# Layer norm of a fused two-layer backbone step: sums by token tile in column groups, root and reciprocal on 96x128, result spread by one-row products

## The chip, the cores and the metric

The kernel runs on one core of a Trainium2 chip. Its engines are TensorE (PE in the profile; PEld is its loading of weights), VectorE (DVE), ScalarE (ACT), GpSimd (POOL) and SyncE (SP); each runs its own list of instructions in order and they meet by semaphores. The metric is the device time of one execution in microseconds (us), and the median of several runs is compared.

## What is computed

A step of a diffusion backbone with two layers for 384 tokens (128 of a prompt, 256 of a latent) of width 1024, all in float32. The layer, cut to what matters:

```python
def layer_norm(x, g, b):
    mu = jnp.mean(x32, axis=-1, keepdims=True)
    var = jnp.mean(jnp.square(x32 - mu), axis=-1, keepdims=True)
    return (x32 - mu) * lax.rsqrt(var + LN_EPS) * g + b

def trunk_layer(x, mod, p, ...):
    shift1, scale1, gate1, shift2, scale2, gate2 = split(mod, 6)
    y, k, v = token_mixer(x * (1 + scale1) + shift1, p, ...)   # projection, attention, pooling, convolution
    x = layer_norm(ALPHA * x + gate1 * y, p['ln1_g'], p['ln1_b'])
    u = x * (1 + scale2) + shift2
    return layer_norm(ALPHA * x + gate2 * hier_moe(u, p), p['ln2_g'], p['ln2_b'])
```

`hier_moe` sends each token to two of 32 gated experts, whose weights are read from memory in each layer. `mod` is a row of SiLU(cond) times `w_mod`, 6144 wide.

## The kernel before

**Layout.** Activations lie turned: `xT` and `uT` hold eight tiles (m = 0 to 7) of 128 channels (partitions) by T = 384 tokens (columns). So a sum over channels is a sum over partitions and over eight tiles, and TensorE makes it: a product with a 128x128 matrix of ones (`C["ones"]`) adds up the partitions and gives the same sum in every partition of a PSUM bank. `ln_t` is a scratch of ten 128x384 tiles. PSUM (`ps`) has eight banks of 512 columns. In the trace each float32 product is two matmul instructions, and a transpose is one.

**A normalisation.** There are two in each layer (`which` 0 and 1), four in all. VectorE (`residual_norm`, L1624) makes z = gate * y + scaled x in place in `uT`, tile after tile (L1640), and adds tiles 0 to 6 together (L1647). TensorE (`layer_norm`, L991) makes the mean from this sum (L994) and the last tile (L996). VectorE subtracts it from each tile, reading PSUM (L1655); ScalarE (`squares_root`) squares each tile (L1331); TensorE adds the squares, eight products of 384 columns (L1003); ScalarE takes the root on 128x384, for which it loads another function table (L1333); VectorE takes the reciprocal on 128x384 (L1662) and scales the eight tiles into `xT` (L1666).

**What follows it.** Next comes u = x * (1 + scale) + shift, even tiles on ScalarE (L1216), odd tiles on VectorE (L1453, `new_u`, after all eight scalings). The shift and scale come from the modulation product (`mod_product`, L796): for each k of eight, four products of 256 or 512 columns with 32-column weights that lie in four column groups of the array. ScalarE copies the result out (L1222), TensorE turns it (`mod_turn`, L808), VectorE adds the bias (L1441) and folds the norm's bias into the shift (L1618, L1621). In the first normalisation TensorE's order is: mean, steps k=0,1 of part 2, squares, steps 2 to 7 of part 2, half of part 3, the turn, the rest of part 3, and then the router product (L1028) on the new u. The first normalisation is followed by routing and the experts (chunks: L1074, L1066, L1081), the second, in layer 0, by the projection of layer 1 (L834), and in layer 1 by the output: ScalarE adds the bias (L1419), TensorE turns the tiles (L1193), both other engines copy them out (L1853, L1423), SyncE stores them. In the second normalisation of layer 0 the modulation product of the next layer (part 0) takes the place of part 2.

**Weights.** SyncE issues the loads into four slots of a ring and a fifth in the arena, each when its slot is free: the w_mod and w_in slots of the next layer behind the last experts (L521, L510), experts behind `gu_ready` and `down_done` of the chunk five before (L559, L561, L566).

## Time and profile before

| | us |
|---|---|
| three runs | 1105.05, 1108.22, 1108.25 |
| median | 1108.22 |
| span of the profiled execution, first to last instruction | 1105.3 |
| TensorE busy in it | 931.0 (84%) |
| VectorE, ScalarE, GpSimd busy | 384.5, 236.6, 178.5 |
| moved by DMA | 321.9 MB, mean 291 GB/s |

The profile is of one execution, and no time of that execution other than its span is given. All times of rows are counted from the span's start. A matmul's end is modelled, since matmuls are pipelined: two that follow each other overlap in their durations, so a group's length divided by its count is the better measure of their rate.

### The profile page before, as it was taken

To read this page: it belongs to the slowest core of one execution; us is meant where nothing else is said; L and a number is where in the kernel's file an instruction comes from. 1 tells how busy PE (TensorE), PEld (TensorE's weight loads), DVE (VectorE), ACT (ScalarE), POOL (GpSimd) and SP (SyncE) were. 2 spreads that over 40 slices of the span, in tenths; PEclk is the share of its full clock that TensorE was granted. 3 is DMA by queue.
4 is the path that set the end of the run, shared out by engine and by line. 5 is a ranking of instruction groups with operands and counts; after the bars stand their busy time and mean duration, and the time that the engine had idled before them with its cause. 6 is when DMAs were issued, how large, how long until landed. Compare 5 with 4: busy or idle time off the path is not lost.

```text
span 1105.3 us, 13927 instructions
## 1 busy us (share of the span) xinstructions
PE 931.0 (84%) x5252; PEld 549.7 (50%) x5252; DVE 384.5 (35%) x921; ACT 236.6 (21%) x565; POOL 178.5 (16%) x214
## 2 busy tenths in 40 slices
PE   4899988994899987798899998899489997779884
PEld 2356455543555543454445654554355554445453
DVE  0257554255211111111646846325611111111146
ACT  1200067032111110111230016703311111011104
POOL 5000000002322222222020000000322222222100
PEclk8899989996999998999999998999699999999998
DMA  9981154078799999997997215317789999999941
GB/s 358 378 308 36 81 193 207 4 293 345 299 412 414 414 413 412 411 386 312 380 336 286 84 41 231 160 41 300 294 339 412 415 414 412 348 415 410 414 182 58
DMA packets 73568, 321.88 MB, mean 291 GB/s; under 512 B 13198, under 2 KB 17638, under 8 KB 49184
## 3 DMA queue, kind: packets, MB, share of 16 engines
q1 hardware_dynamic: 58688, 295.72, 67.3%
q0 software_dynamic: 14816, 25.29, 6.3%
q8 instruction: 42, 0.69, 0.2%
q14 instruction: 22, 0.18, 0.0%
HBM read 321.46 MB, written 23.59 MB: 312 GB/s over the span
## 4 chain that ended last, share of the span: by engine, by line
PE 62%; DMA 16%; SPq 8%; DVE 8%; ACT 3%; issue 3%; POOLq 0%; ACTq 0%; DVEq 0%; POOL 0%
PE ps L834 13%; PE ps L1066 13%; DMA ring<-in_w_up 11%; PE ps L1016 7%; PE ps L1081 6%; PE ps L837 4%; SPq L559 3%; DMA ring<-in_w_mod 3%; SPq L561 2%; PE ps L796 2%; SPq L566 2%; PE ps L1003 2%; PE ps L1074 1%; DMA arena<-u_rows,row_idx 1%; PE ps L1090 1%
## 5 line engine op out<-in xcount | busy, mean ns | idle before, releaser
L1066 PE MATMUL ps<-ring,tail 128*64 128x256 f32 x1760 | 205.1, 384 | 10.4 <-DMA ring<-in_w_up 8.5
L1066 PEld LDWEIGHTS ps<-ring,tail 128*64 128x64 f32 x1760 | 144.0, 139 | 82.9 <-issue 24.5
L834 PE MATMUL ps<-uT,ring 128*128 128x384 f32 x448 | 149.7, 492 | 3.7 <-ACT uT L1216 3.7
L1795 DVE TENSOR_TENSOR arena<-arena,ps 128x128 f32<-128x128 f32 x68 | 19.6, 288 | 364.8 <-ACT arena L1366 364.8
L834 PEld LDWEIGHTS ps<-uT,ring 128*128 128x128 f32 x448 | 85.5, 192 | 60.3 <-issue 5.3
L1081 PE MATMUL ps<-ring,krow 128*64 128x512 f32 x408 | 103.6, 627 | 3.0 <-issue 2.2
L693 POOL DMA_INDIRECT y_pairs<-tail,row_idx x58 | 57.7, 995 | 289.6 <-ACT tail L1391 277.9
L1391 ACT ACTIVATE tail<-ps 128x512 f32<-128x512 f32 x58 | 34.6, 597 | 189.4 <-PE ps L1081 189.4
L688 POOL DMA_INDIRECT arena<-u_rows,row_idx x66 | 68.8, 1043 | 38.0 <-issue 20.1
L1513 DVE SCALAR_TENSOR_TENSOR arena<-arena,dw 128x414 f32<-128x414 f32 x118 | 67.7, 645 | 0.0
L1366 ACT ACTIVATE arena<-ps 128x128 f32<-128x128 f32 x68 | 18.8, 277 | 214.2 <-PE ps L1066 198.0
L1016 PE MATMUL ps<-arena,ring 128*128 128x384 f32 x192 | 62.2, 486 | 0.0
L1074 PE MATMUL ps<-cst,arena 128*128 128x128 f32 x272 | 42.3, 285 | 21.6 <-DMA arena<-u_rows,row_idx 17.8
L1790 DVE COPY tail<-ps 128x512 f32<-128x512 f32 x68 | 46.6, 691 | 37.5 <-PE ps L1074 30.0
L796 PE MATMUL ps<-ring,sT 128*32 128x512 f32 (+1 forms) x512 | 51.2, 540 | 8.5 <-DMA ring<-in_w_mod 8.5
L1128 PE MATMUL ps<-cst,arena 128*128 128x128 f32 x62 | 20.3, 328 | 42.9 <-DVE arena L1795 42.9
L1640 DVE SCALAR_TENSOR_TENSOR uT<-ps,modT,uT 128x128 f32<-128x128 f32 x64 | 23.5, 411 | 83.4 <-PE ps L1016 74.5
L1081 PEld LDWEIGHTS ps<-ring,krow 128*64 128x64 f32 x408 | 29.8, 140 | 41.3 <-issue 41.3
L1066 PE MATMUL ps<-arena,tail 128*64 128x256 f32 x416 | 49.2, 389 | 0.1
L1016 PEld LDWEIGHTS ps<-arena,ring 128*128 128x128 f32 x192 | 36.5, 190 | 25.4
L1074 PEld LDWEIGHTS ps<-cst,arena 128*128 128x128 f32 x272 | 32.1, 146 | 26.9 <-issue 20.9
L1066 PEld LDWEIGHTS ps<-arena,tail 128*64 128x64 f32 x416 | 36.4, 142 | 17.3 <-issue 7.5
(268 smaller groups left out, 979.6 us busy)
## 6 DMA issues: line engine op xcount, KB each, us to landing
ring<-in_w_gate SPq DMA_DIRECT2D x55, 1024.0 KB, 17.1
ring<-in_w_up SPq DMA_DIRECT2D x55, 1024.0 KB, 22.9
ring<-in_w_down SPq DMA_DIRECT2D x55, 1024.0 KB, 23.0
ring<-in_w_mod SPq DMA_DIRECT2D x12, 3072.0 KB, 11.2
arena<-in_w_gate SPq DMA_DIRECT2D x13, 1024.0 KB, 18.3
arena<-in_w_up SPq DMA_DIRECT2D x13, 1024.0 KB, 24.6
arena<-in_w_down SPq DMA_DIRECT2D x13, 1024.0 KB, 25.1
ring<-in_w_mod SPq DMA_DIRECT2D x6, 2048.0 KB, 15.9
```

Source lines behind the costliest of these rows:

```text
L688: pool.indirect_dma_start(xg[:, b, :], None, u_rows, bass.IndirectOffsetOnAxis(ap=idx, axis=0), bounds_check=2 * T - 1, oob_is_err=False). ...
L693: pool.indirect_dma_start(y_pairs, bass.IndirectOffsetOnAxis(ap=idx, axis=0), rows, None, bounds_check=4 * T - 1, oob_is_err=False).then_i ...
L796: last = mm(ps[32 * g_:32 * (g_ + 1), bank, 0:n], sT[:, 2 * k:2 * k + 32], mod_w[MOD_SLOTS[j][u]][:, row, off + g_ * n:off + (g_ + 1) * n] ...
L834: last = mm(ps[:, n % 4, 0:T], slot[s][:, k, c:c + P], uT[:, k, :], start=(k == 0), stop=(k == KD - 1))
L837: last = mm(ps[:, n % 4, 0:AW], uT[:, k, rows * P:(rows + 1) * P], slot[s][:, k, c:c + AW], start=(k == 0), stop=(k == KD - 1))
L1016: last = mm(ps[:, m % 4, 0:T], wt, mixT[:, k, :], start=(k == 0), stop=(k == KD - 1))
L1066: last = mm(ps[W * half:W * (half + 1), b, 0:2 * P].rearrange("p (j f) -> p j f", j=2), xc[:, b, k, :], gate_up_w[s][:, :, k, half * P:(ha ...
L1074: last = tr(ps[:, 5 + b, c * P:(c + 1) * P], xg[:, buf, c * P:(c + 1) * P], ident)
L1081: last = mm(ps[W * half:W * (half + 1), 3 + b, :], hT[:, b, f * W:(f + 1) * W], down_w[s][:, f, half * 512:(half + 1) * 512], start=(f == ...
L1391: fn(yrow[:, i % 2, :], ps[:, 3 + i % 2, :], ID).then_inc(y_rows.sem, 1)
L1513: conv_own.append(own.add(v.scalar_tensor_tensor(cacc[:, c, :], src, wt, cacc[:, c, :], ALU.mult, ALU.add)))
L1790: v.tensor_copy(xc[:, b].rearrange("p (h j) n -> p j h n", h=2), ps[:, 5 + b, :].rearrange("p (j h n) -> p j h n", j=4, h=2)).then_inc(sig ...
```

## The change

**First normalisation (which = 0).** The mean is made as before. The squares are added by `sum_by_tile`: for each m three products of 128 columns, one for each token tile, with 32 columns of ones as weights, in three column groups of the array; they write partitions 0 to 95 of one bank, 128 columns, so token tile g stands in the 32 partitions from 32g. Root and reciprocal work on 96x128. `spread` then multiplies one row of ones with one row of the result for each token tile and so fills banks 1 to 3, and VectorE scales from these three banks. Steps k = 2, 3, 4 of the modulation product are put between the squares' sums, k = 5, 6 behind them, and k = 7 and three steps of part 3 behind the spread. VectorE makes the odd tiles of u between the scalings.

**Second normalisation (which = 1).** The additions of L1647 go; the mean is summed by token tile too, straight from z, copied out by ScalarE with the factor -1/D, and spread to three banks; VectorE centres by an addition from there. The modulation's step 2 stands between the squares and steps 3 to 7 behind the spread. The modulation's bias is added after all eight scalings, not after the sixth. The output's turns use other banks.

The core of the diff:

```diff
+        stat = ln_t[0:32 * NT, 1, 0:2 * P].rearrange("p (b n) -> p b n", b=2)
...
+                def sum_by_tile(bank, x, m):
+                    for g_ in range(NT):
+                        last = mm(ps[32 * g_:32 * (g_ + 1), bank, 0:P], C["ones"][:, 0:32], x[:, g_ * P:(g_ + 1) * P],
+                                  start=(m == 0), stop=(m == KD - 1), tile_position=(0, 32 * g_))
+                    return last
+                def spread(rows):
+                    for g_ in range(NT):
+                        last = mm(ps[:, 1 + g_, 0:P], C["ones"][32 * g_:32 * g_ + 1, :], rows[32 * g_:32 * g_ + 1, :],
+                                  start=True, stop=True)
+                    last.then_inc(stat_spread.sem, 1)
...
                 def layer_norm(which):
-                    wait(z_summed, l, which + 1)
-                    mm(ps[:, 4 * (1 - which), 0:T], C["ones"], ln_t[:, 0, :], start=True, stop=False)
...
+                    if which:
+                        for m in range(KD):
+                            wait(z_ready, l, KD + m + 1)
+                            last = sum_by_tile(0, uT[:, m, :], m)
+                        last.then_inc(norm_sums.sem, 1)
+                        wait(stat_rows, l, 2)
+                        spread(stat[:, 0, :])
...
+                    if ahead < DEPTH:
+                        mod_product(ahead, part, 7, range(2))
                     for m in range(KD):
                         wait(squared, l, which * KD + m + 1)
-                        last = mm(ps[:, 5 - 4 * which, 0:T], C["ones"], ln_t[:, 2 + m, :], start=(m == 0), stop=(m == KD - 1))
-                    last.then_inc(norm_sums.sem, 1)
+                        last = sum_by_tile(5 - which, ln_t[:, 2 + m, :], m)
+                        if m == KD - 1:
+                            last.then_inc(norm_sums.sem, 1)
+                        if ahead < DEPTH and m in ((4,) if which else (2, 4, 6)):
+                            mod_product(ahead, part, 7, range(1 + m // 2, 2 + m // 2) if not which else range(2, 3))
+                    if not which:
+                        mod_product(ahead, part, 7, range(5, 7))
+                    wait(stat_rows, l, 2 * which + 1)
+                    spread(stat[:, 1, :])
...
-                mod_product(l, 2, 7, range(2, KD))
-                mod_product(l, 3, 4, range(KD // 2))
+                mod_product(l, 2, 7, range(KD - 1, KD))
+                mod_product(l, 3, 4, range(KD // 2 - 1))
                 mod_turn(l, 2, 7, D // 4)
-                mod_product(l, 3, 4, range(KD // 2, KD))
+                mod_product(l, 3, 4, range(KD // 2 - 1, KD))
...
                 def squares_root(which):
+                    if which:
+                        wait(norm_sums, l, 3)
+                        fn(stat[:, 0, :], ps[0:32 * NT, 0, 0:P], ID, scale=-1.0 / D).then_inc(stat_rows.sem, 1)
...
-                    fn(ln_t[:, 1, :], ps[:, 5 - 4 * which, 0:T], ACT.Sqrt, bias=epsc[:], scale=1.0 / D).then_inc(root_ready.sem, 1)
+                    fn(stat[:, 0, :], ps[0:32 * NT, 5 - which, 0:P], ACT.Sqrt, bias=epsc[0:32 * NT, :], scale=1.0 / D).then_inc(
+                        root_ready.sem, 1)
...
-                        if 1 <= m < KD - 1:
+                        if not which and 1 <= m < KD - 1:
...
+                        if which:
+                            v.tensor_tensor(by_tile(uT[:, m, :]), spread_rows, by_tile(uT[:, m, :]), ALU.add).then_inc(centred.sem, 1)
...
-                    own.add(v.reciprocal(ln_t[:, 0, :], ln_t[:, 1, :]))
-                    after(own.n)
+                    v.reciprocal(stat[:, 1, :], stat[:, 0, :]).then_inc(stat_rows.sem, 1)
+                    wait(stat_spread, l, 2 * which + 1)
...
+                    if which == 0:
+                        for m in range(4):
+                            scaled(m)
+                        mod_add(l, 2, 7, D // 4)
+                        own.add(mod_scale(l, 3, SC2))
+                        mod_fold("ln1_b", SH2, SC2)
+                        wait(mod_done, l, 2)
+                        next_u(1)
+                        scaled(4)
+                        scaled(5)
+                        next_u(3)
+                        scaled(6)
+                        scaled(7)
+                        next_u(5)
+                        next_u(7)
...
-                    last = tr(ps[:, 2 + n, m * P:(m + 1) * P], uT[:, 4 * h + m, t * P:(t + 1) * P], ident)
+                    last = tr(ps[:, (4 + n) % 8, m * P:(m + 1) * P], uT[:, 4 * h + m, t * P:(t + 1) * P], ident)
```

`DVE_STEPS`, the count of VectorE's own steps in a layer, goes from 209 to 202, and GpSimd's one-time signal for its zeroed block shares the semaphore of another zeroing.

## Rows read from the trace of the kernel before

**Rows 1.** The page, section 4: the chain that ended last, share of span by engine.
```profile
PE 62%; DMA 16%; SPq 8%; DVE 8%; ACT 3%; issue 3%; POOLq 0%; ACTq 0%; DVEq 0%; POOL 0%
```

**Rows 2.** Timeline, first normalisation of layer 0: start us, us, engine line operation, count [idle before].
```profile
232.49 3.77 ACT L1331 ACTIVATE arena<-uT 128x384 f32<-128x384 f32 x8 [39.90 <-DVE uT L1655]
233.07 5.43 PE L1003 MATMUL ps<-arena,cst 128*128 128x384 f32 x16 [0.20 <-ACT arena L1331]
...
236.28 1.28 ACT L1333 ACT_TABLE_LOAD   x1
238.43 4.04 PEld L796 LDWEIGHTS ps<-ring,sT 128*32 128x32 f32 x80 [0.55 <-issue]
238.43 4.52 PE L796 MATMUL ps<-ring,sT 128*32 128x256 f32 x80
238.53 0.58 ACT L1333 ACTIVATE arena<-ps,epsc 128x384 f32<-128x384 f32 x1 [0.97 <-PE ps L1003]
239.15 2.55 DVE L1662 RECIPROCAL arena<-arena 128x384 f32<-128x384 f32 x1 [3.28 <-ACT arena L1333]
...
241.73 1.68 DVE L1666 SCALAR_TENSOR_TENSOR xT<-uT,vec,arena 128x384 f32<-128x384 f32 x3
...
242.88 0.44 PE L808 MATMUL ps<-cst,pool_sums 128*128 128x128 f32 x2
...
243.25 1.93 PE L796 MATMUL ps<-ring,sT 128*32 128x256 f32 x32
...
244.19 3.62 ACT L1216 ACTIVATE uT<-xT,modT 128x128 f32<-128x128 f32 x8 [2.52 <-DVE modT L1621]
...
247.44 4.71 PE L1028 MATMUL ps<-uT,router_w 128*36 128x384 f32 x14 [1.31 <-DVE uT L1453]
```

**Rows 3.** Timeline, second normalisation of layer 0.
```profile
535.77 4.85 PE L1180 MATMUL ps<-cst,arena 128*128 128x128 f32 x42
...
536.06 1.39 DVE L1640 SCALAR_TENSOR_TENSOR uT<-ps,modT,uT 128x128 f32<-128x128 f32 x4 [4.86 <-PE ps L1180]
...
544.34 0.91 PE L994 MATMUL ps<-arena,cst 128*128 128x384 f32 x2 [3.72 <-DVE arena L1647]
...
546.48 3.81 DVE L1655 SCALAR_TENSOR_TENSOR uT<-ps,uT 128x384 f32<-128x384 f32 x8 [1.54 <-PE ps L996]
...
554.68 5.36 PE L796 MATMUL ps<-ring,sT 128*32 128x512 f32 x48
...
563.43 20.88 PE L834 MATMUL ps<-uT,ring 128*128 128x384 f32 x64 [2.02 <-ACT uT L1216]
```

**Rows 4.** Timeline, second normalisation of layer 1, the end of the program.
```profile
1071.94 5.52 PE L1180 MATMUL ps<-cst,arena 128*128 128x128 f32 x48
...
1084.15 3.81 DVE L1655 SCALAR_TENSOR_TENSOR uT<-ps,uT 128x384 f32<-128x384 f32 x8 [2.37 <-PE ps L996]
...
1093.98 4.32 DVE L1666 SCALAR_TENSOR_TENSOR xT<-uT,vec,arena 128x384 f32<-128x384 f32 x8
1094.63 4.32 ACT L1419 ACTIVATE uT<-xT,vec 128x384 f32<-128x384 f32 x8 [3.27 <-DVE xT L1666]
```

**Rows 5.** Windows: stretch, length, TensorE busy (count), granted clock, DMA share, GB/s.
```profile
547.00:548.00 1.00, 1.00 (x8) 0.50 1.06 442
```

**Rows 6.** Windows of all engines around the first experts: clock, DMA share, GB/s last.
```profile
276.00:282.00 6.00, 6.00 (x43) 4.11 (x41) 1.38 (x2) 1.77 (x2) 3.79 (x4) 0.75 0.21 57
282.00:290.00 8.00, 6.61 (x50) 4.03 (x47) 1.56 (x4) 1.15 (x3) 2.04 (x2) 1.00 0.80 309
```

**Rows 7.** Layer 1's w_in loads: issues by first and last start; one to landing.
```profile
L510 SPq DMA_DIRECT2D ring<-in_w_in x7: 368/508/16453, 531.4 to 561.7; - x7
...
ring<-in_w_in SPq DMA_DIRECT2D x1, 2048.0 KB, 27.0
```

**Rows 8.** Single lines, whole trace: ns min/median/max, first and last start.
```profile
L1608 DVE RECIPROCAL rms<-rms x2: 227/227/227, 182.0 to 703.9; 128x12 f32<-128x12 f32 x2
L1366 ACT ACTIVATE arena<-ps x68: 277/277/278, 282.3 to 1060.5; 128x128 f32<-128x128 f32 x68
```

75 lines of the change are left out of this document (43 added, 32 removed).

## The prediction

> **What bounds the kernel now.** I read the chain of work that ended last first: 62% of it is TensorE, 16% DMA, 8% SyncE's queue, 8% VectorE [rows 1]. The four normalisations (two a layer) lie on that chain between large TensorE stages, so I read the timeline of each next, then the clock, then the DMA, to see whether a stage that ends earlier lets the next one start earlier.
>
> In the first normalisation of layer 0, VectorE centres eight tiles, ScalarE squares them from 232.49, one behind, and is done at 236.26. TensorE adds up the squares from 233.07 in 5.43 us (0.68 a tile) and ends at 238.50, 2.2 us after the last square. Then root 0.58, reciprocal 2.55, and the scaling from 241.73. The modulation can start at 244.19 and the router product runs to 252.15, its last 14 matmuls 0.336 us apart: there TensorE is the limit [rows 2]. Layer 1 repeats this 522 us later.
>
> In the second normalisation of layer 0 the additions L1647 sit between VectorE's residual steps: z begins at 536.06. TensorE has ended the y tiles at 540.62 and stands idle for 3.7 us until the additions are done, at 544.34; centring starts at 546.48, the modulation products for the next layer end at 560.04, the projection begins at 563.43 [rows 3]. The one in layer 1 is the end of the program: centring 1084.15, scaling 1093.98, ScalarE's output steps from 1094.63 [rows 4].
>
> **First normalisation (twice).** The sum of the mean is unchanged, so the squares still end at 236.26. Grouped sums: three products of 128 columns in three column groups. The nearest row is L796, four products in four groups, 80 instructions in 4.52 us, 56 ns each [rows 2]. One product of 256 columns alone would take 0.68 x 256/384 = 0.45 us; four take 0.45 together, so groups overlap. Six instructions at that rate are 0.34 us a tile. Low end: a third of 0.68, 0.23; high end: no overlap, 0.68. I take 0.34, the rate of the nearest row. Three modulation steps (k=2 to 4, 0.45 each) are put between; a square comes each 0.47 us, so two tiles plus one step cost 1.13 of 0.94. TensorE falls behind a little and ends some 0.6 after the last square, at 236.9. That hides nothing further: the root waits for its table load, 236.28 plus 1.28, which stood under TensorE's lag before [rows 2]. So the sums bring 0.95 us here (238.53 to 237.58), not 1.6.
>
> Root on 128 columns: 0.58 before, 0.28 by an ACTIVATE of 128 columns from PSUM [rows 8]; it ends at 237.9. Reciprocal: 12 columns took 0.227, 384 took 2.552 [rows 2, 8], that is 6.25 ns a column, so 128 cost 0.95: done at 238.87. The spread is new: six instructions. The trace has 0.115 us for one of 128 columns (4.85/42 [rows 3]), and 0.21 us of fill (two in 0.44 [rows 2]): 0.90. Low end 0.45, if the three row positions overlap; high end 1.6, at half clock. I take 0.90: scaling starts at 239.85, 1.9 earlier.
>
> Scaling now reads its factor from PSUM, in three banks. Centring, which reads PSUM, takes 0.466 a tile ((3.81-0.55)/7; an instruction of it is 0.55 [rows 4]); scaling from SBUF 0.53 ((4.32-0.61)/7, 0.61 being one of them [rows 4]). I take 0.47; the other end is 0.53 or a little more for the three-piece pattern, 0.5 us a norm. Four scalings end at 241.75.
>
> TensorE's wait for the reciprocal stands before step k=7 of the third modulation part, three steps of the fourth and the turn; VectorE's bias addition and both engines' modulation wait for them. After the spread: k=7 and three steps, 1.8 us, to 241.6. From the end of products to the start of the modulation was 1.24 us (242.95 to 244.19 [rows 2]), so it now starts at 242.85. VectorE's first odd tile is ready at 243.5 and not after all eight scalings. Five steps more (0.48 each, 1.93/4) end at 244.3; the router product follows at TensorE's own pace, 16 x 0.336 = 5.4, to 249.75. The tiles arrive 0.5 to 2 us ahead of it. **Gain 2.4 us each, 4.8 in two.**
>
> A rule of the Trainium skill (TensorEngine Tiling (Array Packing), Tiling Modes) speaks against this: changing the tiling mode drains TensorE. The rows show a pause of 0.55 us in the weight loads where the tile shape changes and none in the matmuls [rows 2]. By the rule, taken at 0.55 for the some ten changes that are added in all, the whole saving would be 12.7-5.5 = 7.2 us.
>
> **Second normalisation, layer 0.** Without L1647 z is paced by VectorE, 0.69 a tile (1.39 for two [rows 3]): the last is ready at 541.6. The y tiles hold TensorE until 540.62; the mean sums of eight tiles then take 8 x 0.34 = 2.7, to 543.35 (ends 542.4 and 546.1). ScalarE's copy of 96x128 is 0.28, the spread 0.90, the handoffs 0.1: centring starts at 544.65, 1.8 earlier. Products k=0,1 (8 instructions each, 0.112 us apiece by 5.36/48 [rows 3]) end at 546.4, and the first square is by then ready; with k=2 between, the sums end at 550.1. The squares end at 549.0, the table at 550.3, the root at 550.65, the reciprocal at 551.65, the spread at 552.55. Behind it TensorE has k=3 to 7, 40 x 0.112 = 4.5, to 557.0, against 560.04. The rest keeps its 3.39 us: projection at 560.4. **Gain 3.0.** VectorE is done scaling at 556.3, before it is wanted.
>
> That is allowed by the loads: the projection's first weights were issued at 531.4 and took 27.0 us, so they lie there at 558.4 [rows 7]. More than 5.0 us can't be had here.
>
> **Second normalisation, layer 1.** The y tiles end at 1077.46 [rows 4]; sums to 1080.2, copy and spread to 1081.5: centring 1081.55, 2.6 earlier, more than in layer 0 since TensorE was at its slow clock there. Squares end 4.36 later, table, root, reciprocal and spread as above (1.28, 0.35, 1.0, 0.9): scaling at 1089.45, 4.5 earlier. With 0.47 in place of 0.53 a tile, 0.4 more at the last: **gain 4.9**.
>
> The rest costs nothing: the output's banks (4+n)%8 are free by then, and the zero semaphore is only shared. Fewer VectorE steps (DVE_STEPS) are the reciprocals and additions already counted.
>
> **Sum.** 4.8 + 3.0 + 4.9 = 12.7 us. The profiled span is 1105.3, at the lowest run (1105.05); the median is 1108.22, and nothing shown tells the 2.9 us between them. From the span the sum gives 1092.6, from the median 1095.5. I forecast medians: **1095.5 us**.
>
> **The rivals.**
> (a) *The gain of the first normalisations is taken back by the weight stream.* Against it: DMA is 0.21 busy while the experts begin and 0.80 after [rows 6], so its later loads wait for TensorE to free slots and start earlier with it. For it: it is saturated afterwards and sets the ends. Without 4.8: 1100.3. Chance 0.12.
> (b) *The clock of the second normalisation, layer 0.* TensorE was granted 0.50 (1.2 GHz) at 547 after standing idle for 3.7 us, and 1.00 again before the products k=2 to 7, whose 0.112 us is the full rate [rows 3, 5]. Now it is idle 1.5 us ahead of the spread and lightly loaded before it. If k=3 to 7 and the spread run at 1.2 GHz, 5.4 us more: 1100.9. Chance 0.08.
> (c) *The groups don't overlap*: 0.68 a tile. The first normalisations then have their sums at 239.85 and the router product at 252.0: 0.15 each. Layer 0's second one has centring at 547.5, squares summed at 555.7, products to 562.5: 2.4 lost. The last gains 0.4 at scaling's pace and 0.9 before it. In all 0.8 lost: 1109.0. L796 speaks against it. Chance 0.10.
> (d) *Slower: the clock of the first normalisations.* Thin products in place of dense ones, then idleness for the reciprocal; TensorE is granted 1.2 GHz and stays there through nine modulation steps (+4.2), the router product (+5.4) and the spread (+0.7): 10.3 in each layer, and (b)'s 5.4 and 0.8 at the end besides, 26.8 in all. 1108.2-12.7+26.8 = 1122.3. It decides from 16 us of such loss, the 12.7 saved and the 3.3 that can be told. Against it: L796's thin products kept full pace. Chance 0.06.
>
> **How the numbers follow.** Forecast 0.64, (a) 0.12, (b) 0.08, (c) 0.10, (d) 0.06. The forecast's own range is 1090 to 1099.5: spread at 0.45, sums at 0.23 and the lowest run's 2.9 below; spread at half clock and scaling at 0.53 above. With (a) and (b) the range is 1089.5 to 1102.5; (c), (d) and tails stay out. 0.3% is 3.3 us, about what a measurement can tell here: faster 0.84 (forecast, a, b), same 0.10 (c), slower 0.06 (d).
>
> **What would show it.** Sums right behind each square, the root directly behind the table load, a reciprocal of some 0.95 us, a spread of some 0.9, no L1647 additions in the second normalisation, and the router product without a hole. Wrong: a granted clock of 0.50 in the router product or in k=3 to 7; sums of 0.68 a tile; the experts' first matmuls earlier but their last at the old time; or a scaling slowed by the three-bank pattern.

## The result

| | before | changed |
|---|---|---|
| median of the runs, us | 1106.96 (four, 1105.05 to 1108.25) | 1101.15 (four, 1100.24 to 1102.16) |
| span of the profiled execution, us | 1105.3 | 1099.1 |
| ratio on record, 95% interval | | 0.9927 (0.9904 to 0.995) |

The changed kernel is faster by 5.8 us in its median, 0.5%. The ratio on record is an estimate of its own and not the quotient of these two medians, which is 0.9948; by the ratio it is 0.7%, some 8 us. Run again beside other runs of the kernel before (`after_again`, below) the ratio was 0.9910 (0.9892 to 0.9927), 10 us. The prediction was 1095.5, in a range of 1089.5 to 1102.5. So sign and range held, and the size was 12.7 us predicted against 6 to 10 measured. The rest of the document asks where the missing part went. Two executions of the experiments below, one of fifth_early (1438.18 us) and one of combo (1936.05 us), were in a slow state and are left out of every median and ratio.

### The profile page after: what moved, and what is told of

Read it like the earlier page. It is cut to its first block, busy times and chain, and to the rows that moved or that the text cites. A ratio compares the mean times of both kernels' runs of the same rounds, so it can differ in the third digit from the quotient of the medians.

```text
span 1099.1 us, 14411 instructions
## 1 busy us (share of the span) xinstructions
PE 922.4 (84%) x5504; PEld 546.4 (50%) x5504; DVE 371.8 (34%) x909; ACT 236.4 (22%) x567; POOL 178.3 (16%) x214
## 4 chain that ended last, share of the span: by engine, by line
PE 61%; DMA 17%; SPq 9%; DVE 6%; ACT 5%; issue 2%; POOLq 0%; ACTq 0%; DVEq 0%; POOL 0%
PE ps L836 14%; PE ps L1097 12%; DMA ring<-in_w_up 11%; PE ps L1047 8%; PE ps L1112 6%; PE ps L839 4%; SPq L561 3%; PE ps L798 3%; SPq L563 3%; DMA ring<-in_w_mod 3%; SPq L568 3%; DMA arena<-u_rows,row_idx 2%; PE ps L1105 1%; ACT arena L1365 1%; PE ps L1121 1%
## 5 line engine op out<-in xcount | busy, mean ns | idle before, releaser
L1097 PE MATMUL ps<-ring,tail 128*64 128x256 f32 x1760 | 205.2, 384 | 14.5 <-DMA ring<-in_w_up 12.7
L798 PE MATMUL ps<-ring,sT 128*32 128x512 f32 (+1 forms) x512 | 55.4, 550 | 8.2 <-DMA ring<-in_w_mod 8.2
L1105 PEld LDWEIGHTS ps<-cst,arena 128*128 128x128 f32 x272 | 32.5, 147 | 32.0 <-issue 25.7
L1159 PEld LDWEIGHTS ps<-cst,arena 128*128 128x128 f32 x62 | 8.6, 138 | 71.0 <-DVE arena L1860 71.0
## 6 DMA issues: line engine op xcount, KB each, us to landing
ring<-in_w_mod SPq DMA_DIRECT2D x12, 3072.0 KB, 11.4
```

Source lines behind the costliest of these rows:

```text
L798: last = mm(ps[32 * g_:32 * (g_ + 1), bank, 0:n], sT[:, 2 * k:2 * k + 32], mod_w[MOD_SLOTS[j][u]][:, row, off + g_ * n:off + (g_ + 1) * n] ...
L1097: last = mm(ps[W * half:W * (half + 1), b, 0:2 * P].rearrange("p (j f) -> p j f", j=2), xc[:, b, k, :], gate_up_w[s][:, :, k, half * P:(ha ...
L1105: last = tr(ps[:, 5 + b, c * P:(c + 1) * P], xg[:, buf, c * P:(c + 1) * P], ident)
```

## The profile after

The chain of work that ended last, by engine. Against [rows 1] VectorE's share of the chain went from 8% to 6%, and ScalarE's from 3% to 5%.

```profile
PE 61%; DMA 17%; SPq 9%; DVE 6%; ACT 5%; issue 2%; POOLq 0%; ACTq 0%; DVEq 0%; POOL 0%
```

**First normalisation of layer 0**, the timeline that answers to [rows 2]. The columns are start us, length us, engine, line, operation, buffers, shapes and count, then the idle time before and what ended it.

```profile
232.35 3.77 ACT L1365 ACTIVATE arena<-uT 128x384 f32<-128x384 f32 x8 [39.91 <-DVE uT L1701]
...
236.15 1.28 ACT L1367 ACT_TABLE_LOAD   x1
...
237.44 0.36 ACT L1367 ACTIVATE arena<-ps,epsc 96x128 f32<-96x128 f32 x1
237.84 0.95 DVE L1709 RECIPROCAL arena<-arena 96x128 f32<-96x128 f32 x1 [2.11 <-ACT arena L1367]
...
238.84 0.50 PE L1003 MATMUL ps<-arena,cst 1*128 1x128 f32 x6 [1.19 <-DVE arena L1709]
...
239.40 2.19 DVE L1714 SCALAR_TENSOR_TENSOR xT<-uT,vec,ps 128x384 f32<-128x384 f32 x4 [0.61 <-PE ps L1003]
...
242.44 3.84 ACT L1247 ACTIVATE uT<-xT,modT 128x128 f32<-128x128 f32 x8 [2.08 <-DVE modT L1656]
...
243.79 5.35 PE L1059 MATMUL ps<-uT,router_w 128*36 128x384 f32 x16
```

The root follows the table load directly. The modulation starts at 242.44 (244.19 before), the router product ends at 249.14 (252.15 before) and has no hole, at 0.33 us an instruction. Locally the change brings 3.0 us here, more than the 2.4 predicted.

**From there to the experts.** First the timeline of the changed kernel: SyncE's issue of the gate weights for the fifth and sixth chunk, GpSimd's gather of the experts' input rows (`u_rows`), TensorE's first transposes of them.

```profile
264.87 0.33 SPq L561 DMA_DIRECT2D ring<-in_w_gate  x1
268.31 1.10 POOL L690 DMA_INDIRECT arena<-u_rows,row_idx  x1 [9.40 <-DVE row_idx L1828]
...
275.22 1.94 PE L1105 MATMUL ps<-cst,arena 128*128 128x128 f32 x8 [8.86 <-DMA arena<-u_rows,row_idx]
...
282.12 0.33 SPq L561 DMA_DIRECT2D ring<-in_w_gate  x1
```

In it, the time from issue to landing of the three stores into `u_rows` (one per token tile) that the gather needs:

```profile
DMA to landing us min/median/max: 6.1/6.6/7.0
```

The same rows of the timeline of the kernel before:

```profile
265.00 0.33 SPq L559 DMA_DIRECT2D ring<-in_w_gate  x1
271.32 1.10 POOL L688 DMA_INDIRECT arena<-u_rows,row_idx  x1 [9.40 <-DVE row_idx L1763]
...
275.72 2.02 PE L1074 MATMUL ps<-cst,arena 128*128 128x128 f32 x8 [6.35 <-DMA arena<-u_rows,row_idx]
...
282.38 0.33 SPq L559 DMA_DIRECT2D ring<-in_w_gate  x1
```

And the landing of its stores:

```profile
DMA to landing us min/median/max: 4.1/4.5/4.6
```

The gather is issued 3.0 us earlier, and the transposes that wait for it start 0.5 us earlier; TensorE waits 8.86 us in place of 6.35. The fifth chunk's weights are issued at the same time in both, 0.13 us apart. SyncE holds them until the stores have landed (`u_stored`); the stores are issued 3.0 us earlier but take 6.1 to 7.0 us in place of 4.1 to 4.6, since they share the DMA with the third and fourth chunk's weights, which moved by less (242.62 to 241.31 for the third). So the gather, which is earlier, falls into the fifth chunk's weights. The Trainium skill (Trainium Kernel Development and Optimization, Key Constraints) states that transfers issued from the queues of SyncE, ScalarE and GpSimd run on the same 16 DMA engines and interleave; the landing times here agree.

**Second normalisation of layer 0**, the answer to [rows 3]:

```profile
541.34 1.95 PE L996 MATMUL ps<-uT,cst 128*32 128x128 f32 x48
544.22 3.81 DVE L1699 TENSOR_TENSOR uT<-ps,uT 128x384 f32<-128x384 f32 x8 [1.97 <-PE ps L1003]
...
551.30 0.50 PE L1003 MATMUL ps<-arena,cst 1*128 1x128 f32 x6 [2.12 <-DVE arena L1709]
551.73 6.20 PE L798 MATMUL ps<-ring,sT 128*32 128x512 f32 x40
...
561.31 5.16 PE L836 MATMUL ps<-uT,ring 128*128 128x384 f32 x10 [2.02 <-ACT uT L1247]
```

The windows there, as in [rows 5]: TensorE's busy share and count, and the granted clock third from the end.

```profile
553.00:554.00 1.00, 1.00 (x12) 0.28 (x8) 1.00 (x3) 0.00 (x0) 0.00 (x0) 0.50 1.04 385
563.00:564.00 1.00, 1.00 (x3) 0.65 (x2) 0.66 (x4) 0.98 (x3) 1.00 (x3) 0.50 0.98 352
```

From the end of the y tiles to the projection it is 19.90 us in place of 22.81, 2.9 less. The sums of the mean are 0.244 us a tile (1.95/8), but steps k=3 to 7 took 6.20 us: TensorE stood idle for 2.12 us ahead of the spread, and the granted clock was 0.50 (1.2 GHz) behind it. The window in the head of the projection shows 0.50 too.

**The last normalisation**, the answer to [rows 4]:

```profile
1080.42 3.81 DVE L1699 TENSOR_TENSOR uT<-ps,uT 128x384 f32<-128x384 f32 x8 [1.97 <-PE ps L1003]
...
1081.59 3.67 PE L996 MATMUL ps<-arena,cst 128*32 128x128 f32 x48 [1.22 <-ACT arena L1365]
...
1086.10 0.36 ACT L1367 ACTIVATE arena<-ps,epsc 96x128 f32<-96x128 f32 x1
...
1088.05 4.29 DVE L1714 SCALAR_TENSOR_TENSOR xT<-uT,vec,ps 128x384 f32<-128x384 f32 x8 [0.61 <-PE ps L1003]
...
1090.94 4.72 PE L1224 MATMUL ps<-cst,uT 128*128 128x128 f32 x24 [2.95 <-ACT uT L1454]
```

Centring starts 3.7 us earlier, scaling 5.9, and from the end of the y tiles to the end of the span it is 21.48 us in place of 27.84: 6.4 less, of 4.9 predicted.

**The span cut at four events** tells where the gain stayed. wout is the output projection ahead of the first normalisation; "experts" runs from its end to the last expert's end; "between" from there to the next wout's end, with the second normalisation of layer 0 in it; "end" from the last expert of layer 1 to the end. Each kernel of this study has its row, from its profiled execution (us).

| kernel | to first wout | experts, layer 0 | between | experts, layer 1 | end | span |
|---|---|---|---|---|---|---|
| before | 230.1 | 298.7 | 223.3 | 313.5 | 39.7 | 1105.3 |
| changed | 229.9 | 299.6 | 222.4 | 313.8 | 33.4 | 1099.1 |
| after_again | 229.0 | 299.8 | 222.1 | 313.4 | 33.5 | 1097.9 |
| first_new | 228.1 | 299.5 | 225.8 | 314.0 | 42.5 | 1109.9 |
| second_new | 231.3 | 299.1 | 220.1 | 313.5 | 33.4 | 1097.4 |
| last_new | 227.7 | 297.7 | 223.8 | 313.4 | 33.6 | 1096.1 |
| fifth_late | 228.9 | 299.9 | 222.1 | 314.5 | 34.0 | 1099.5 |
| fifth_early | 231.6 | 299.2 | 219.9 | 313.0 | 34.7 | 1098.5 |
| fill | 230.8 | 299.6 | 219.0 | 313.5 | 33.5 | 1096.4 |
| table | 231.5 | 299.5 | 219.8 | 312.8 | 33.6 | 1097.2 |
| combo | 228.8 | 298.8 | 219.6 | 310.7 | 32.8 | 1090.6 |
| slots_ahead | 229.2 | 298.2 | 220.5 | 310.0 | 33.5 | 1091.5 |
| best | 230.3 | 298.9 | 219.5 | 310.8 | 33.1 | 1092.6 |

The first column lies ahead of everything that the kernels differ in, and it spreads over 3.9 us: one span can't be compared with another more finely, and a stage is read by its own length. The changed kernel against the one before: -0.2, +0.9, -0.9, +0.3, -6.3. Of the 3.0 us that each first normalisation saves, nothing is left at the end of the experts. How finely a stage can be read: before, second_new and last_new have the same first normalisations and the same experts, and their stages lie between 297.7 and 299.1 us in layer 0 and between 313.4 and 313.5 in layer 1.

## The experiments

Three theories of why the experts' end doesn't follow. **A**, the prediction's: the later weights wait for TensorE to free slots, so they start earlier with it, and only the late gather is in the way. **B**: the gain is spent before the experts, since the gather competes with the fifth chunk's weights; with them out of the way it comes through. **C**: the stage is its bytes at full rate plus the time in which the DMA engines stand idle; an earlier TensorE helps as far as it makes them stand idle less. Ratios are against the kernel before in the same batch, with 95% intervals. The first four ran in one batch (before 1109.07), the next four in a second (1109.08), the last three in a third (1108.60).

**Which normalisations pay.** In three kernels a table picks the form of each normalisation, by layer and `which`; the counts of semaphores follow from it. All three compute the whole. This is second_new; in first_new the two first normalisations have True and the two second ones False, in last_new only `(1, 1)` has True.

```diff
+NEW = {(0, 0): False, (0, 1): True, (1, 0): False, (1, 1): True}
...
-                    if which:
+                    new = NEW[l, which]
+                    if which and new:
```

> Both first normalisations are as before the change, both second ones as after it. Theory A (the first normalisations end 3.0 us earlier but the weights of the fifth expert are still issued at the old time, so the row gathers behind them land at nearly the old time, and nothing is left at the end of the layer): about 1101.3, the time of the changed kernel, within 0.8. Theory B (each normalisation keeps a share of what it saved and the shares add up): the two first ones brought 1 us each, so about 1103.3. In the trace the first expert's transposes should start at 275.7 as before the change.

> Both first normalisations as after the change, both second ones as before it. Theory A: the time of the kernel before, 1107, less at most 0.7 (0.26 us is all that the experts' later loads were earlier). Theory B: about 1105. The router product should end at 249.1 and the gather of the first expert's rows should take some 6.5 us instead of 4.2 in either theory; they differ in the time at the end of the experts.

> Only the second normalisation of the last layer is as after the change, the other three as before. Theory A: the end of the program alone carries the gain, 6.3 us by the two traces less what the clock does: about 1101.0, no slower than 1102 . Theory B: at most two thirds of the gain, 1103 or more. If this kernel is as fast as the changed one, the other three normalisations brought nothing.

| kernel | median, us | ratio | gain by the ratio, us |
|---|---|---|---|
| second_new | 1098.41 | 0.9907 (0.9885 to 0.9929) | 10.3 (7.9 to 12.8) |
| first_new | 1107.93 | 0.9987 (0.9974 to 0.9999) | 1.4 (0.1 to 2.9) |
| last_new | 1102.96 | 0.9947 (0.9931 to 0.9963) | 5.9 (4.1 to 7.7) |

The last column is 1109.07 times one minus the ratio. The second normalisations alone give as much as the whole change gave in either of its measurements. The first ones alone give 1.4 us, of 4.8 forecast. The last one gives 5.9, and the difference of second_new and last_new leaves 4.4 for the second one of layer 0, of 3.0 forecast. Either gain is known to some 2 us, so 4.4 is rough, but the profiles say the same: "between" is 220.1 us long in second_new and 223.8 in last_new. It passes through. In the profile of first_new the experts' stages are 299.5 and 314.0 long, none shorter than before. Its span, 1109.9, is no sign that it is slower: its old form of the last normalisation met a low clock in this execution, and the squares' sums took 8.14 us for the 5.43 of [rows 2], as its timeline has it:

```profile
1087.19 8.14 PE L1046 MATMUL ps<-arena,cst 128*128 128x384 f32 x16 [1.20 <-ACT arena L1390]
```

**The fifth chunk's weights behind the gathers** (A and B against C).

```diff
                     elif i == 4:
                         wait(mod_rows, l, 4)
-                        wait(u_stored, l, NT, alone=True)
+                        for b in range(XBUFS - 1):
+                            wait(xg_loaded[b], l, 1)
+                        wait(xg_loaded[XBUFS - 1], l, 1, alone=True)
```

> The changed kernel, but SyncE issues the fifth expert's weights (slot 2) when the first four row gathers have landed, not when the rows are stored. Theory A: the gathers land some 3 us after their issue at 268.3, the first expert's transposes start at about 271.8 instead of 275.2, and since the later loads are issued as TensorE frees slots, the saturated stream and the end of the experts come 3 us earlier in each layer: about 1095. Theory C (the end of the experts is set by the bytes of the stream, whose start is the fifth expert's load and not the experts' first product): the transposes start earlier but the last expert ends where it did, 1101 within 1, or later, since the fifth load is now issued 6 us later.

Median 1102.26, ratio 0.9938 (0.9921 to 0.9956). Its timeline in layer 1, first transposes and the issues of the fifth and sixth chunk's weights:

```profile
792.18 1.09 PE L1107 MATMUL ps<-cst,arena 128*128 128x128 f32 x4 [4.74 <-DMA arena<-u_rows,row_idx]
...
796.64 0.33 SPq L561 DMA_DIRECT2D ring<-in_w_gate  x1
801.57 0.33 SPq L561 DMA_DIRECT2D ring<-in_w_gate  x1
```

The changed kernel's two issues:

```profile
786.46 0.33 SPq L561 DMA_DIRECT2D ring<-in_w_gate  x1
804.00 0.33 SPq L561 DMA_DIRECT2D ring<-in_w_gate  x1
```

The transposes start 41.2 us behind wout in place of 44.8, so the first half of B is shown: without the weights beside it the gather is fast. But the stage is 314.5 us long in place of 313.8. The sixth chunk's weights start 2.4 us earlier (1.4 counted from wout's end, 50.6 for 52.0), as A has it, the fifth's 10.2 later, and in the first 60 us behind wout the DMA engines stand idle for longer (18.0 us, 15.5 in the changed kernel). The sixth's earlier issue brings nothing while the fifth's bytes are still to come, so the second half of B falls, and A isn't the whole of it: C's condition is needed beside it. Of the 3.6 us that the transposes gained only 1.4 reached the sixth's issue, for a reason that has to do with the clock and is shown further down.

**The fifth chunk's weights without waiting for the stores.**

```diff
                     elif i == 4:
-                        wait(mod_rows, l, 4)
-                        wait(u_stored, l, NT, alone=True)
+                        wait(mod_rows, l, 4, alone=True)
```

> The changed kernel, but the fifth expert's weights (slot 2) are issued as soon as the modulation has freed the slot (about 244), not when the rows of u are stored (264.9). Theory A with C's correction (the end of the experts hangs on when the first five experts' bytes are in and the sixth is issued, both together): the fifth weights are through before the gathers at 268.3, which then land in 3 to 4 us; first transposes at 271.8, sixth load at 278.8 instead of 282.1, last expert 3 us earlier in each layer: ratio to the kernel before near 0.987. Theory D (the stream is held by something later than the start, so a start 3 us earlier is lost whatever is loaded): last expert as before, 299 us after the end of the output projection in layer 0 and 313.6 in layer 1, ratio 0.993.

Median 1100.35, ratio 0.9906 (0.9878 to 0.9933). The landing of the stores in layer 0:

```profile
DMA to landing us min/median/max: 9.0/10.8/11.6
```

And from its timeline the first transposes:

```profile
275.46 1.09 PE L1104 MATMUL ps<-cst,arena 128*128 128x128 f32 x4 [7.43 <-DMA arena<-u_rows,row_idx]
```

The weights are issued at 246.30 in place of 264.87, but the stores now take 9.0 to 11.6 us and the gather waits for them, to 272.17. The stages are 0.4 and 0.8 us shorter than in the changed kernel, little more than profiles of one stage differ (0.4 us in layer 1 between the changed kernel and after_again). The interval can't be told from the changed kernel's. The wait for the stores only orders the traffic; the bytes stay.

**Three of the modulation's steps moved ahead, to free weight slots sooner** (C expects a gain in the experts' stage; the expectation's D, by which a later limit holds the end, expects none). It doesn't separate C from A, since the gather meets less traffic too and TensorE starts earlier.

It has the edit of fifth_early, and part 3 lies in bank 6 (the router's product in bank 4), so that its steps k=0 to 2 can run ahead of part 2's k=3 to 7:

```diff
-                            mod_product(ahead, part, 7, range(1 + m // 2, 2 + m // 2) if not which else range(2, 3))
+                        if not which and m in (2, 4, 6):
+                            mod_product(l, *{2: (2, 7, [2]), 4: (3, 6, [0]), 6: (3, 6, [1])}[m])
...
-                        mod_product(ahead, part, 7, range(5, 7))
+                        mod_product(l, 3, 6, [2])
+                        mod_product(l, 2, 7, [3])
...
-                mod_product(l, 2, 7, range(KD - 1, KD))
-                mod_product(l, 3, 4, range(KD // 2 - 1))
+                mod_product(l, 2, 7, range(4, KD))
+                mod_product(l, 3, 6, [3, 4])
...
-                mod_product(l, 3, 4, range(KD // 2 - 1, KD))
+                mod_product(l, 3, 6, range(5, KD))
```

> The changed kernel with the fifth expert's weights early, and the first normalisation's modulation steps in another order: part 3's k=0 to 2 come before part 2's k=3 to 7, so that the first slot is free some 4 us earlier and the DMA engines, idle then, begin the third expert's weights at about 237 instead of 241. Theory C (the stage from the output projection to the last expert is as long as its bytes at the full rate and the idle time of the DMA engines; starting the experts earlier helps only as far as it takes idle time away): idle time of the first 60 us down from 15 to 11 or 12, first transposes at 272, the stage 3 us shorter in each layer, 296.5 and 310.5; ratio 0.987. Theory D (a later limit holds the end): 299 and 313 us as before, ratio 0.993.

> The changed kernel itself once more, beside the next two and under the same runs of the kernel before. Every theory: ratio to the kernel before 0.990 to 0.995; in the profile 299.6 and 313.8 us from the end of the output projection to that of the last expert, with the DMA engines idle for some 15 us of the first 60 of each.

Slots_ahead: median 1093.53, ratio 0.9874 (0.9855 to 0.9892). After_again, the changed kernel on the same chip: median 1099.83, ratio 0.9910 (0.9892 to 0.9927). So it is some 4 us faster by the ratios, whose intervals just touch, and 6.3 by the medians. The third chunk's weights are issued 7.4 us behind the end of wout (747.98) in place of 11.4 (751.96), and the first transposes start 41.5 us behind it in place of 44.8. The issues of slots_ahead for the third and the sixth chunk (the sixth 48.9 us behind wout, 52.0 in the changed kernel by its 804.00 above):

```profile
755.41 0.33 SPq L561 DMA_DIRECT2D ring<-in_w_gate  x1
...
796.84 0.33 SPq L561 DMA_DIRECT2D ring<-in_w_gate  x1
```

And the changed kernel's for the third:

```profile
763.36 0.33 SPq L561 DMA_DIRECT2D ring<-in_w_gate  x1
```

The windows of 60 us behind wout in layer 1 (stretch, length, granted clock, DMA share, GB/s), and the rest of the stage, of the kernel before:

```profile
752.08:812.08 60.00, 0.83 0.73 286
812.08:1065.57 253.49, 0.99 1.00 399
```

The changed kernel:

```profile
751.96:811.96 60.00, 0.80 0.74 287
```

Fifth_late:

```profile
750.98:810.98 60.00, 0.80 0.70 275
```

Slots_ahead, with the rest of its stage:

```profile
747.98:807.98 60.00, 0.86 0.79 304
807.98:1058.02 250.04, 0.99 1.00 400
```

Behind the first 60 us the DMA share is 1.00 at 399 or 400 GB/s in both; only the share of the head differs, 0.73, 0.74, 0.70 and 0.79. Five hundredths of 60 us are 3.0 us, and slots_ahead's stage is 3.7 shorter. Over all kernels, idle DMA time being the stage less the summed busy time of the 16 engines over 16; the last two columns are counted in layer 1, from wout's end to the issue of the sixth chunk's gate weights, and from there to the end of the stage:

| kernel | layer 1: stage | DMA idle in it | difference | layer 0: difference | sixth issued | stage behind it |
|---|---|---|---|---|---|---|
| before | 313.5 | 17.0 | 296.5 | 279.1 | 52.3 | 261.2 |
| changed | 313.8 | 17.0 | 296.7 | 280.0 | 52.0 | 261.7 |
| first_new | 314.0 | 17.9 | 296.2 | 279.4 | 52.1 | 262.0 |
| fifth_late | 314.5 | 19.4 | 295.2 | 278.5 | 50.6 | 263.9 |
| fifth_early | 313.0 | 17.4 | 295.6 | 279.6 | 51.3 | 261.7 |
| slots_ahead | 310.0 | 13.7 | 296.3 | 279.4 | 48.9 | 261.2 |
| combo | 310.7 | 14.7 | 296.0 | 279.8 | 49.4 | 261.3 |
| best | 310.8 | 15.1 | 295.8 | 279.8 | 49.0 | 261.8 |

In all thirteen profiles layer 1's difference lies between 295.2 and 296.7, while the idle time changes by 5.7. The bytes moved in the stage are the same in the changed kernel and the one before (118.3 and 118.2 MB in layer 1, 112.0 in layer 0). These first columns alone are bookkeeping: they say that a stage can only get shorter by idle DMA time, and not what shortens that time.

The last two columns do. In twelve of the thirteen profiles the stage ends 261.1 to 262.0 us behind the issue of the sixth chunk's weights (245.6 to 247.9 in layer 0), and in the thirteenth, fifth_late, 263.9 (251.2). So A's chain holds, with one condition: when the sixth's weights are issued sets when the stage ends, provided that the first five chunks' are in by then. SyncE issues them 0.1 us behind the end of TensorE's product of gate and up for the first chunk, which frees the slot. Ahead of that issue the DMA engines have nothing to do: in slots_ahead they are busy from 5 to 15 us behind wout (share 1.00, 0.68 in the changed kernel) and idle for it from 35 to 45 (0.21, 0.85 in the changed kernel). Loading earlier moved the idle time; what shortened it is the first product, which ended earlier.

That product hangs on the granted clock as much as on the transposes. Its rows, of slots_ahead in layer 1 and layer 0:

```profile
792.47 4.28 PE L1099 MATMUL ps<-ring,tail 128*64 128x256 f32 x32
...
274.93 5.33 PE L1099 MATMUL ps<-ring,tail 128*64 128x256 f32 x32
```

And of fifth_late in layer 1:

```profile
795.57 5.91 PE L1099 MATMUL ps<-ring,tail 128*64 128x256 f32 x32
```

Fifth_late and slots_ahead start it alike in layer 1, 44.6 and 44.5 us behind wout, but in slots_ahead the granted clock is 1.00 again from 46 us on and in fifth_late only from 49 us, so that it takes 5.91 us in one and 4.28 in the other (4.66 in the changed kernel, 4.25 before). So of the 4.5 us between their stages 1.7 lie in the sixth's issue and 2.7 behind it, where the fifth's bytes were late. In layer 1 the clock is back by 46 us in slots_ahead, combo and best, the three with a stage under 311 us; in layer 1 of every other kernel, and in layer 0 of these three, it is back at about 49. This is also why slots_ahead brings only 1.4 us in layer 0 (299.6 to 298.2): the product takes 5.33 us there and the sixth's weights are issued at 51.1 us. And combo has a stage of 310.7 without the steps moved. So of slots_ahead's 3.7 us in layer 1 some 1.6 (5.91 less 4.28) are an estimate of what the clock gave; whether the edit brings the clock back sooner, or one execution happened to have it, no run shows.

**Idle products to hold the clock in the second normalisation of layer 0.** Eight products into a bank whose content nobody reads: four ahead of the wait for the reciprocal, four around the turn behind the steps.

```diff
+                def keep_busy(n):
+                    for _ in range(n):
+                        mm(ps[:, 5, 0:LAT], C["ones"], C["cos"], start=True, stop=True)
...
+                    elif ahead < DEPTH:
+                        keep_busy(4)
                     wait(stat_rows, l, 2 * which + 1)
...
+                    keep_busy(1)
                     mod_turn(l + 1, 0, 6, 0)
+                    keep_busy(3)
```

> The changed kernel with eight idle products (256 columns, into a bank that nobody reads) on TensorE in the second normalisation of layer 0: four ahead of its wait for the reciprocal, one ahead of and three behind the turn of the modulation. If the granted clock of 0.50 in the modulation steps k=3 to 7 (6.20 us instead of 4.5) and at the head of the projection comes from TensorE's idleness before them: steps 4.5, from the y tiles' end to the projection 18.2 us instead of 19.9, from there to the end of the next output projection 188.5 instead of 190.6, 3.5 us in all, which pass on since they shift a whole layer with its loads: ratio near 0.990. If the clock is not set by that, the two stretches stay at 19.9 and 190.6.

Median 1098.70, ratio 0.9887 (0.9858 to 0.9916). From its timeline, steps k=3 to 7 and the projection's head:

```profile
552.60 4.50 PE L798 MATMUL ps<-ring,sT 128*32 128x512 f32 x40
...
560.49 4.75 PE L836 MATMUL ps<-uT,ring 128*128 128x384 f32 x14 [0.72 <-ACT uT L1255]
```

The window in the steps, which answers to the changed kernel's first one above:

```profile
553.00:554.00 1.00, 1.00 (x16) 0.34 (x12) 1.00 (x3) 0.00 (x0) 0.00 (x0) 1.00 1.03 385
```

The clock is held, the steps take the 4.50 us that the prediction had, and from the y tiles to the projection it is 18.21 us (19.90 in the changed kernel). From the projection's start to the next wout's end it is 188.9 us, 190.7 in the changed kernel. With the filling, the steps took 4.50 us in all three kernels that have it (fill, combo, best). Without it they took 6.12 to 6.20 us in five (the changed kernel, after_again, second_new, fifth_late, fifth_early), with a granted clock of 0.50 in them. But slots_ahead has the same code and the same idle spell at this place and kept its clock:

```profile
549.26 0.50 PE L1002 MATMUL ps<-arena,cst 1*128 1x128 f32 x6 [2.12 <-DVE arena L1711]
549.68 4.50 PE L797 MATMUL ps<-ring,sT 128*32 128x512 f32 x40
```

So the 1.7 us are the clock's, but the idle spell of 2.1 us alone doesn't settle whether it falls. That filling the spell holds the clock agrees with three profiles and isn't proven by them. Of slots_ahead's gain in its profile some 1.6 us ("between", 220.5 for 222.1) came from here and not from its edit. The cold head of the projection is no mark of the change: it is 191.2 in first_new with the old form, 190.7 in last_new, 188.7 before, and 188.3 in second_new, 188.1 in fifth_early with the new form. Fill's interval holds one of the changed kernel's ratios, 0.9910, and not the other, 0.9927.

**The root's function table loaded ahead of the squares.**

```diff
                 def squares_root(which):
+                    fn(root_one[:], epsc[:], ACT.Sqrt)
```

> The changed kernel with one root of a 128x1 constant on ScalarE ahead of each normalisation's squares, where ScalarE is idle, so that the root's table is loaded there. If the squares need no table of their own, no load stands between the last square and the root. Root in the last normalisation at some 1085.4 instead of 1086.1 (the sums end there), the end 0.7 us earlier; 0.7 in the second normalisation of layer 0; nothing kept of the first ones. Ratio near 0.991 to 0.992. Rival: the table is loaded again for the squares, or the copies, and this costs 1.3 us more for each load.

Median 1096.91, ratio 0.9875 (0.9852 to 0.9898). Its timeline in the last normalisation, centring, root and the output's transposes:

```profile
1078.32 3.81 DVE L1701 TENSOR_TENSOR uT<-ps,uT 128x384 f32<-128x384 f32 x8 [1.96 <-PE ps L1004]
...
1083.34 0.36 ACT L1369 ACTIVATE arena<-ps,epsc 96x128 f32<-96x128 f32 x1 [0.65 <-PE ps L997]
...
1088.18 5.30 PE L1225 MATMUL ps<-cst,uT 128*128 128x128 f32 x24 [2.95 <-ACT uT L1456]
```

And ahead of it the projection of layer 1:

```profile
560.70 5.51 PE L837 MATMUL ps<-uT,ring 128*128 128x384 f32 x11 [2.13 <-DMA ring<-in_w_in]
```

No load stands between squares and root, and the squares run under the root's table. From centring to root it is 5.02 us, 5.68 in the changed kernel. In the last normalisation that isn't kept (end 33.6 for 33.4), as the output's transposes took 5.30 us for 4.72. In layer 0 the y tiles to the projection is 17.80 us, and the projection now waits for its own weights: that is the bound of 5.0 us from [rows 7], met to the tenth (22.81 - 17.80 = 5.01). Of the 2.1 us by which it is shorter than in the changed kernel only 0.7 were expected of the table. Steps k=3 to 7 took 4.64 us for 6.20, at a granted clock of 1.00: with the root earlier, TensorE's idle spell ahead of the spread is 1.46 us for 2.12. By the ratios table gains 3.9 us on after_again, and the two intervals overlap slightly.

**All together.** Combo is fifth_early, fill and table in one; best is slots_ahead, fill and table.

> The three edits together: fifth weights early, the eight idle products, the root's table ahead. If they hold and are independent: 6 + 3.5 + 1.4 us less than the changed kernel, ratio near 0.983. If the start of the experts isn't what sets their end: near 0.988.

> slots_ahead with the root's table loaded ahead and the eight idle products in the second normalisation of layer 0. If each does what its own run showed: 2 us less there than slots_ahead, 0.7 at the end, ratio 0.983 to 0.985, the fastest of all.

Combo: median 1096.14, ratio 0.9883 (0.9860 to 0.9905). Best: median 1093.06, ratio 0.9852 (0.9837 to 0.9866), 15.5 us below the kernel before, and its interval lies below the changed kernel's in both measurements. It can't be told from slots_ahead alone (0.9855 to 0.9892), nor which part of combo brings its gain; its profiled execution, with a span of 1090.6, was the fastest of its runs by 3.3 us.

## Why the prediction was right or wrong

**What held.** The four normalisations were on the chain, and each got shorter by about what the steps said or more. Its size:

| term | predicted | measured |
|---|---|---|
| sums, us a tile | 0.34 | 0.244 |
| spread | 0.90 | 0.50 |
| root on 96x128 | 0.28 | 0.36 |
| reciprocal | 0.95 | 0.95 |
| scaling of eight tiles, from 4.32 | some 3.9 | 4.29 |
| first normalisation, to the router's end | 2.4 | 3.0 |
| second of layer 0, to the projection | 3.0 | 2.9 |
| k=3 to 7 in it | 4.5 | 6.20 |
| last normalisation | 4.9 | 6.4 |

**The term that failed** is the 4.8 us of the first normalisations. First_new measured 1.4 (0.1 to 2.9), and in the profiles of the changed kernel nothing of it is left at the experts' end. The prediction answered its own rival (a) with: "its later loads wait for TensorE to free slots and start earlier with it". The wait was right: the sixth's weights are issued 0.1 us behind the first product, and the stage's end follows that issue. What it took for granted is that TensorE's first product is 2.4 us earlier because the router product is. It was not: the sixth's weights were issued 0.3 us earlier in each layer. Between the two lie the stores, the gather and the granted clock, which the prediction did not follow, and the saturated stream behind the issue, at a DMA share of 1.00, had no room to give back. Rival (a) was given 0.12, and its time, 1100.3, is within 1 us of the measured median. Its mechanism, a stream that is saturated and sets the ends, is true from the sixth's issue on.

**Luck.** The forecast's own range was 1090 to 1099.5, and 1101.15 lies outside it; the stated range held because (a) and (b) were taken into it. Both rivals were priced within 1 us of the result (1100.3 and 1100.9), so the time alone doesn't tell which one came. Two of the signs that the prediction gave for being wrong did come: a granted clock of 0.50 in k=3 to 7, and the experts' first matmuls earlier but their last at the old time (528.7 us before and 529.5 after in layer 0, 1065.6 and 1065.7 in layer 1). The other terms hid part of the miss: the last normalisation gave 6.4 for 4.9.

**Where the local gain went first.** Of 3.0 us at the router, 2.5 were gone at the first transposes of layer 0 (275.72 to 275.22) and 2.2 in layer 1 (797.50 to 796.74, with 774.19 to 771.20 at the router). Of the 0.5 and 0.8 left, another part went in the first product, more of which lay ahead of the clock's return: 4.66 us for 4.25 in layer 1. The order "stores, then fifth weights, then gather" stands in the code, so it could have been seen that moving the gather by 3 us puts it nearer to the weights.

**The second normalisation of layer 0: two errors that cancel.** Sums and spreads were faster by 1.6 us together (0.8 in the mean's sums, 0.4 in each spread), and k=3 to 7 slower by 1.7. Rival (b) was thus true of the steps, at 1.7 us and not the 5.4 of its price: the clock rose again before they ended, and the spread ran at its full speed. The cause is the clock: the windows show 0.50 in the steps, and in the kernels that kept 1.00 (fill, combo, best, slots_ahead) they took 4.50. That it fell here is no fixed cost of the change, since slots_ahead kept it. Of the local 2.9 us the changed kernel's profile keeps only 0.9 at the next wout's end ("between", 222.4 for 223.3), as from the projection on it took 190.7 us for 188.7.

**The last normalisation** is the larger part of what was kept. It was sized 1.5 too small, by the spread (twice 0.4), the sums of the mean (0.8, less what else is there) and the output's transposes, 4.72 us in place of 5.12. Scaling from three PSUM banks gave nothing back.

**The rivals that did not come.** (c), groups that don't overlap: 0.244 against the 0.69 of six such instructions alone (5.52/48 x 6, by [rows 4]), so they overlap 2.8 times. (d): in both layers TensorE was granted 1.00 from the first sum of squares to the end of the router product, which ran at 0.33 us an instruction.

**The drain.** The sums and the modulation steps have one tile shape (128*32), so the added changes of shape lie around the spreads and ahead of the mean's sums. There the matmuls follow each other: the steps start 0.43 us behind a spread of 0.50 (551.30 and 551.73), the sums at 541.34 with the transposes ahead of them ending at 541.41. The local gains are no less than those of the sum that left a drain out, but for 0.1 us. The rule of the Trainium skill (TensorEngine Tiling (Array Packing), Tiling Modes), priced at 5.5 us in all, didn't show here.

**What stays open.** Second_new brings 10.3 us by its ratio and 7.9 by its profile (1105.3 to 1097.4); the changed kernel 5.8 to 10. Whether the new first normalisations cost a little in it, or nothing, the intervals don't tell. Nor was it settled why the head of the projection is granted 1.2 GHz in some kernels and not in others, or what decides when the full clock comes back at the first experts. No kernel has the steps moved and the fifth's weights at their old place, so what the moved steps bring by themselves is open.

## What to carry to other kernels

Ahead of a stretch in which DMA runs at its full rate, look for the transfer whose issue starts that stretch, and for what frees its slot. Here it is the sixth chunk's weights and TensorE's first product. A saving ahead of it is worth what it takes off the time of that issue, if everything before it is in by then, and nothing else: 3.0 us at the router became 0.3. So follow the whole way, each small store and gather past the large loads that share its way, and the first product at the clock that it is granted. A low share of busy DMA there is not room for the engine but time that the stretch can't get back. A saving at the end of a program, or in front of a stage whose inputs already lie there, was kept here as far as the ratios tell (5.9 and some 4.4 us).

## What the runs showed of the hardware

- The six instructions of three one-row products (row positions 0, 32 and 64 of the array) take 0.50 us together, where six full ones take 0.69 by the rate above: they overlap too.
- TensorE, lightly loaded and then idle for 2.1 us, went to a granted clock of 0.50 in five kernels' profiles and kept 1.00 in a sixth with the same code there (slots_ahead). With four products of 256 columns in the gap it kept 1.00 in three of three, and with a gap of 1.46 us in one (table).
- At the first experts the full clock came back about 46 or about 49 us behind the output projection, and the same product of 32 matmuls, started at 44.5 and 44.6 us, took 4.28 and 5.91 us.
- VectorE's pace is the same from three PSUM banks as from SBUF in a scaling with three operands (4.29 and 4.32 us for eight tiles), while centring, with two, took 3.81.
- Three small stores took 4.5, 6.6 and 10.8 us from issue to landing (medians), by how much weight traffic they met.
